# First mixer of a two-block model: logarithms moved behind exponentials, both score maxima taken together, projection jobs spread over other steps, four chunk states made earlier

## What is computed

```python
def gqa_attention(q, k, v):
    ...
    def one_block(qblk):
        s = jnp.einsum('bqkgd,bskd->bkgqs', qblk, k, preferred_element_type=jnp.float32) * scale
        pr = jax.nn.softmax(s, axis=-1)
        return jnp.einsum('bkgqs,bskd->bqkgd', pr.astype(v.dtype), v)
    ...

def gla_chunk_scan(q, k, v, log_f):
    ...
    def step(state, inp):
        qi, ki, vi, gi = inp
        b = jnp.cumsum(gi.astype(jnp.float32), axis=2)
        diff = b[:, :, :, None, :] - b[:, :, None, :, :]
        decay = jnp.exp(jnp.where(lower, diff, -jnp.inf))
        A = jnp.einsum('bhtd,bhsd,bhtsd->bhts', qi.astype(jnp.float32), ki.astype(jnp.float32), decay)
        o_intra = jnp.einsum('bhts,bhse->bhte', A, vi.astype(jnp.float32))
        o_inter = jnp.einsum('bhtd,bhde->bhte', qi.astype(jnp.float32) * jnp.exp(b), state)
        b_last = b[:, :, -1:, :]
        k_dec = ki.astype(jnp.float32) * jnp.exp(b_last - b)
        new_state = state * jnp.exp(b_last[:, :, 0, :])[..., None] + \
            jnp.einsum('bhsd,bhse->bhde', k_dec, vi.astype(jnp.float32))
        return new_state, o_intra + o_inter
    ...

def hgrn2_bidirectional(hq, hf_f, hf_b, hi, hg, lb, out_norm):
    ...
    def gates(fpre, lbd):
        f = lbd + (1.0 - lbd) * jax.nn.sigmoid(fpre.astype(jnp.float32))
        f = f.reshape(B, S, HG_HEADS, HG_DK)
        return 1.0 - f, jnp.log(f)
    ...
```

## Time and profile before

| | us |
|---|---|
| median of 3 runs | 3444.86 |
| the three runs | 3439.9 to 3446.48 |
| the profiled execution, its own time | 3439.18 |
| span of the profiled execution | 3437.3 |
| PE busy | 3080.0 (90%) |
| DVE busy | 2068.4 (60%) |
| ACT busy | 740.9 (22%) |
| POOL busy | 661.1 (19%) |
| the first mixer's attention steps, from the first scores to the last transposes | 157.3 to 310.3 |
| its gated heads, from the first turned keys to the last sum | 345.2 to 506.4 |

### The profile page before, as it was taken

How to read it: one execution, slowest core, us unless ns; L and a number is a source line. 1 busy time by engine, 2 the same in 40 slices (tenths; PEclk the granted TensorE clock), 3 DMA queues, 4 the chain that set the end, 5 groups by cost and what they waited for, 6 DMA issues and landing times. The chain is left out here.

```text
span 3437.3 us, 30881 instructions
## 1 busy us (share of the span) xinstructions
PE 3080.0 (90%) x11312; PEld 1738.6 (51%) x11312; DVE 2068.4 (60%) x4458; ACT 740.9 (22%) x1638; POOL 661.1 (19%) x649
## 2 busy tenths in 40 slices
PE   8999899898888787878777889999999988999998
PEld 3454554433333333333333334536864467878887
DVE  5666731776666777776666318436567777456433
ACT  2134220222222222222222220112111133121000
POOL 0211000344443544444444100000000000000000
PEclk9999899999999999998999999999999999999999
DMA  5765211899999999999999532112235554212222
GB/s 195 250 203 171 74 50 61 329 421 421 421 422 422 417 419 421 413 416 416 418 418 412 222 114 77 49 37 101 86 128 214 209 212 177 78 63 92 91 86 74
DMA packets 118680, 799.23 MB, mean 233 GB/s; under 512 B 13728, under 2 KB 16416, under 8 KB 31872
## 3 DMA queue, kind: packets, MB, share of 16 engines
q0 software_dynamic: 91312, 619.09, 44.7%
q1 hardware_dynamic: 27216, 178.15, 14.5%
HBM read 767.83 MB, written 29.36 MB: 232 GB/s over the span
## 5 line engine op out<-in xcount | busy, mean ns | idle before, releaser
L1312 PE MATMUL po<-pair,diag 128*128 128x512 f32 x2048 | 975.2, 632 | 215.6 <-ACT diag L1395 215.1
L1489 DVE SCALAR_TENSOR_TENSOR pair<-pair,h_tm 128x1024 f32<-128x1024 f32 x512 | 619.2, 1226 | 323.5 <-DMA pair<-in_peer_uv,idx 317.5
L1312 PEld LDWEIGHTS po<-pair,diag 128*128 128x128 f32 x2048 | 404.8, 202 | 758.9 <-issue 473.4
L1205 POOL DMA_INDIRECT pair<-in_peer_uv,idx x512 | 588.7, 1150 | 955.4 <-PE po L1312 661.4
L1388 ACT ACTIVATE ge<-a 128x2 f32<-128x2 f32 (+2 forms) x178 | 36.4, 204 | 930.3 <-DVE pair L1489 930.2
L1911 PE MATMUL acc<-a,ring 128*128 128x512 f32 x512 | 220.9, 592 | 0.0
L1395 ACT ACTIVATE diag<-ident,wt 128x128 f32<-128x128 f32 x512 | 169.1, 392 | 40.9 <-DVE wt L1493 40.9
L1911 PEld LDWEIGHTS acc<-a,ring 128*128 128x128 f32 x512 | 97.3, 190 | 122.0 <-issue 122.0
L1622 PE MATMUL bank<-hT,ring 128*128 128x256 f32 x592 | 139.8, 379 | 0.0
L1622 PE MATMUL bank<-hT,weight_sums 128*128 128x256 f32 x592 | 139.8, 379 | 0.0
L1598 DVE TENSOR_TENSOR weight_sums<-ring 128x512 f32<-128x512 f32 x53 | 36.7, 692 | 168.8 <-DMA ring<-in_w_fc 151.7
(11 more groups left out here) (492 smaller groups left out, 4172.5 us busy)
## 6 DMA issues: line engine op xcount, KB each, us to landing
ring<-in_w_fc SPq DMA_DIRECT2D x62, 1024.0 KB, 4.9
mg<-in_ada_w POOLq DMA_DIRECT2D x96, 512.0 KB, 5.3
tab<-s_tables SPq DMA_DIRECT2D x16, 1664.0 KB, 6.5
ring<-in_w SPq DMA_DIRECT2D x15, 1024.0 KB, 4.9
first<-in_w_first SPq DMA_DIRECT2D x14, 1024.0 KB, 7.7
other<-in_w_first SPq DMA_DIRECT2D x14, 1024.0 KB, 5.0
s_tables<-weight_sums POOLq DMA_DIRECT2D x8, 1664.0 KB, 6.5
s_tables<-table POOLq DMA_DIRECT2D x8, 1664.0 KB, 6.1
```

Of the source, the lines that this page charges most:

```text
L1205: pool.indirect_dma_start(out=pair[:, at, :], out_offset=None, in_=core.dram["peer_uv"][:, :], in_offset=bass.IndirectOffsetOnAxis(ap=idx[ ...
L1312: last = pe.matmul(po[:, t % 2, half * 512:(half + 1) * 512], diag[:, at, :], pair[:, at, D + half * 512:D + (half + 1) * 512], start=firs ...
L1489: dve.scalar_tensor_tensor(row, row, 1.0, h_tm[:, t, :], ALU.mult, ALU.mult, accum_out=a[:, s:s + 1]).then_inc(dotted, 1)
```

## The change

Nothing is added to or taken from the work; only its order changes, in five places.

1. `beside`: the twelve jobs now stand in the steps 0 to 4, 6, 7, 8, 10, 11, 12 and 14; the steps 5, 9 and 13, which have `mix`, and step 15 have none.
2. In the steps with `mix` it stands behind the transposes.
3. ScalarE's two logarithms stand behind the exponentials of units 3 and 5.
4. VectorE takes both maxima of a step first, then one row of `modulate`, both `scale`, and two rows.
5. In the gated heads TensorE makes `key_values(h, 0, 4)` right behind `score(h)`, ahead of the filler job, and VectorE makes `states(h, 0, 4)` right behind `mask(h)`, ahead of the next head's `gates_one`. Two of the four rows of `modulate` ahead of `gates_two(0)` move to heads 0 and 1, one each.

```diff
--- before.py
+++ after.py
@@ -487,7 +487,7 @@
 
         def beside(i):
 
-            return JOB_HV + i - i // 4 - 1 if i % 4 else None
+            return None if i in (5, 9, 13, 15) else JOB_HV + i - sum(i > x for x in (5, 9, 13))
 
         def rows(d, i):
             return (0, GB * (i + 1)) if d == 0 else (GB * i, GC)
@@ -599,11 +599,11 @@
                               start=True, stop=True).then_inc(scored, 1)
                 if beside(i) is not None:
                     job(beside(i))
-                if i >= 5 and i % 4 == 1:
-                    mix(i // 4 - 1)
                 if i:
                     transposes(2 * i - 2)
                     transposes(2 * i - 1)
+                if i >= 5 and i % 4 == 1:
+                    mix(i // 4 - 1)
             transposes(30)
             transposes(31)
             job(JOB_GATE0 + 4)
@@ -685,8 +685,8 @@
                 turn_keys(h)
                 filler(1 if h < 2 else 0)
                 score(h)
+                key_values(h, 0, 4)
                 filler(1)
-                key_values(h, 0, 4)
                 inside(h)
                 filler(1 if h < 2 else 0)
                 key_values(h, 4, NCH - 1)
@@ -742,9 +742,6 @@
                 take(JOB_F + i, kf[:, i // GH, i % GH, :], ACT.Sigmoid).then_inc(taken, 1)
             for h in range(GH):
                 take(JOB_HQ + h, hq[:, h, :], ACT.Silu).then_inc(taken, 1)
-            for d in range(2):
-                act.wait_ge(kept, GH * (d + 1))
-                act.activation(lf[:, d, :, :], lf[:, d, :, :], ACT.Ln).then_inc(logged, 1)
 
             def copy(u):
                 j, a, t = place(u)
@@ -778,6 +775,9 @@
                 act.activation(prob[:, u % 4, :], bank[:, u % 2, :], ACT.Exp, bias=stat[:, 0, u % 8:u % 8 + 1],
                                scale=AD ** -0.5, accum_out=stat[:, 1, u % 8:u % 8 + 1]).then_inc(expd, 1)
                 i = u // 2
+                if u in (3, 5):
+                    act.wait_ge(kept, GH * (u // 2))
+                    act.activation(lf[:, u // 2 - 1, :, :], lf[:, u // 2 - 1, :, :], ACT.Ln).then_inc(logged, 1)
                 if u % 2 and beside(i) is not None:
                     take_later(beside(i))
                 if u % 2 and i:
@@ -939,16 +939,17 @@
                 step(dve.reciprocal(stat[:, 2, u % 8:u % 8 + 1], stat[:, 1, u % 8:u % 8 + 1]))
                 dve.tensor_scalar(prob[:, u % 4, :], prob[:, u % 4, :], stat[:, 2, u % 8:u % 8 + 1], None, ALU.mult).then_inc(scaled, 1)
 
-            for u in range(32):
-                dve.wait_ge(scored, u + 1)
-                if u >= 8:
-                    dve.wait_ge(scaled, u - 7)
-                step(dve.tensor_reduce(stat[:, 0, u % 8:u % 8 + 1], bank[:, u % 2, :], AX.X, ALU.max))
-                dve.tensor_scalar(stat[:, 0, u % 8:u % 8 + 1], stat[:, 0, u % 8:u % 8 + 1], -AD ** -0.5, None, ALU.mult).then_inc(maxed, 1)
-                if u >= 1:
-                    scale(u - 1)
-                modulate(1 + u % 2)
-            scale(31)
+            for i in range(16):
+                for u in (2 * i, 2 * i + 1):
+                    dve.wait_ge(scored, u + 1)
+                    if u >= 8:
+                        dve.wait_ge(scaled, u - 7)
+                    step(dve.tensor_reduce(stat[:, 0, u % 8:u % 8 + 1], bank[:, u % 2, :], AX.X, ALU.max))
+                    dve.tensor_scalar(stat[:, 0, u % 8:u % 8 + 1], stat[:, 0, u % 8:u % 8 + 1], -AD ** -0.5, None, ALU.mult).then_inc(maxed, 1)
+                modulate(1)
+                scale(2 * i)
+                scale(2 * i + 1)
+                modulate(2)
 
             step = Steps(dve, h_step)
 
@@ -1058,19 +1059,18 @@
             dve.memset(kk[:, :, :, :, :], 0.0).then_inc(zeroed, 1)
             dve.wait_ge(zeroed, 2)
             gates_one(0)
-            modulate(4)
+            modulate(2)
             gates_two(0)
             for h in range(GH):
                 mask(h)
+                states(h, 0, 4)
                 if h < 2:
                     up(ups.pop(0))
                 if h + 1 < GH:
                     gates_one(h + 1)
                 if h < 2:
                     up(ups.pop(0))
-                states(h, 0, 4)
-                if h < 2:
-                    modulate(4)
+                    modulate(5)
                     up(ups.pop(0))
                 states(h, 4, NCH - 1)
                 if h + 1 < GH:
```

## The result

The changed kernel takes 3398.7 us (median of 4 runs, 3396.42 to 3403.37) where the kernel before takes 3442.38 beside it: a ratio of 0.9873, 95% interval 0.9861 to 0.9886, so 43.7 us or 1.3% faster. Measured once more with the last experiments, it took 3400.83 against 3441.55, a ratio of 0.9881 (0.9866 to 0.9896), 40.7 us less. The forecast was 3406, 39 us less.

A forecast was written before the change was run, and what follows sets the result against it. TensorE was taken to bound the stage, waits costing idle time and slow-clock matmuls. Attention -21.4 and heads -17.6 make -39.0: from 3439.18 to 3400.2 us, plus 5.7 for the median, 3405.9; range 3395 to 3418.

The forecast's parts named there:

- Attention, -21.4: Attention steps: 152.97 us become 130.1 as TensorE's waits go, less 1.5 for a slow stretch behind step 15; -20.3 to -22.9.
- The way to head 0, -2.3: Ahead of head 0: two fewer VectorE rows cut TensorE's wait for turned keys from 3.49 to 1.2 us.
- Head 0, -1.6: Gated head 0, scores to next scores: 39.4 us become 37.8, with a new wait of 3.1 for late states.
- Head 1, -5.1: Gated head 1: 41.97 us become 36.9, with a 2.6 us wait for `up` and 1.1 of slow job.
- head 2, -7.6: Gated head 2: 40.58 us become 33.0, from a 4.43 us wait and 3.2 of slow clock behind it.
- head 3, -1.0: Gated head 3: its wait of 1.18 us goes, 1.0 us saved.
- A: Gated heads: VectorE takes most of the gain; heads give -8, total -29.4, 3415 us; chance 0.16.
- B: Attention's end and heads: clock stays up, no slow jobs behind waits; total -44 to -46, 3400 us; chance 0.11.
- C: Attention: rows of ada_w arrive late, costing 5 to 7 us; total -33, 3412 us; chance 0.05.
- D: Attention and heads: slower, TensorE stays at 1.2 GHz after a wait; 3452 us if 46 us run slow; chance 0.03.
- E: Whole kernel: nothing changes, because TensorE's idle time comes back in another stage; chance 0.03.

The follow-up runs named there:

- the maxima apart: Changed kernel with VectorE's old order in the attention (maximum, earlier unit's scale, rows of ada_w, unit by unit): 3402.78 us, 0.9893 of the kernel before.
- the jobs as before: Changed kernel with the attention's jobs in their old steps and the mix ahead of the transposes again: 3403.79 us, 0.9887 of the kernel before.
- job 30 in the last step: Changed kernel with job 30 and its ScalarE copy moved ahead of the last two transposes and their copies: 3398.64 us, 0.9867 of the kernel before.
- the attention's edits alone: Kernel before with only the first four of the five edits, gated heads left as they were: 3422.18 us, 0.9952 of the kernel before.

## Why the prediction was right, point by point

- **The place.** It was TensorE's waits ahead of scores and key values, and what was saved on TensorE came out at the end: 39.4 on the touched stretch, 40.7 and 43.7 on medians. The forecast of 3406 lies 7.2 above the 3398.7: 2.5 because the sum took the first median of before (3444.86) as base, where the one beside the changed kernel was 3442.38, 0.4 for the sum itself, and 4.3 outside the touched stretch. That the sum is right to 0.4 is partly luck: the misses below are 2.6 us to the one side and 2.2 to the other.
- **Attention, -21.4.** Measured -21.37. Its parts too: 130.38 for 130.1, step 15's wait 2.49 for 2.7 to 2.8, the mix step 5.66 for 5.62, job 30 slow by 1.2 for 1.5 (with the last transposes, slow as well, 1.8). The argument that a mix step has work enough to cover the chain held. The prediction did not count ScalarE's copies in step 15, the first of which ends some 0.5 us ahead of the scale. The role of the maxima was told incompletely: without them each mix step waits 0.97 for a scale, and step 15 over 2 us more.
- **The way to head 0, -2.3.** Measured -3.87. The wait is 1.20 as forecast; what I had left in the sum was the slow clock behind the old wait of 3.49 (turned keys 1.76 to the next row, now 0.93; job 4.27, now 3.53). Behind a wait of 1.20 the matmuls ran at full speed.
- **Head 0, -1.6.** Measured -0.92, and here the working was off. I had job 37 wait 0.9 for the `up`, behind a slow first job, and then one wait of 3.1 at `across`. With the clock up TensorE was there 2 us earlier, waited 3.22 for the `up`, ran the job slowly (5.27) and then waited 2.09 more for the late states. I had also not seen that five rows in a burst are one more than there are buffers: the fifth waits 0.69 for its transfer (0.53 in head 1), with the `up` and the states behind it. Nor had I the wait of 1.57 ahead of job 39. The new waits of heads 0 and 1 are 8.65 us, for which the prediction's text says 5.0 (its own 0.9, 3.1 and 2.6 make 6.6); the 2 us above that are about what TensorE was earlier.
- **Head 1, -5.1; head 2, -7.6; head 3, -1.0.** Measured -5.34, -7.97 and -1.45. In head 1 the sum is nearer than its parts: the wait was 1.77 for 2.6, with no slow job behind it, where 1.1 was counted, but key values and the first job were 1.6 us slow, which I had not foreseen. Heads 2 and 3 run without idle time, at full clock.
- **Missing.** The output jobs became 1.53 slower: the wait ahead of them is 2.95 in both kernels, and the slow matmuls behind it were 3.1 now and 1.5 before. The sum had no term for it, and the difference is nothing that the change does to these jobs: in the runs with the maxima apart and with the jobs as before, nothing was lost there.
- **Rivals.** A did not come: heads 0 and 1 are bound by VectorE, as it said, but gave 6.3 between them, and head 2 gave all of its gain. (Its own terms give 7.1 for the heads, not 8.) B came for the start of head 0 only. C is seen in the 0.69 and 0.53 of the heads; in the attention rows waited for a transfer once, for 0.20. D: the clock is 1.00 over the attention; denser work brought a higher clock, not a lower one. E: nothing came back but the 1.53 of the output jobs.

By the Trainium skill's rule on transposes (TensorE: Matmul & The Clock Gate, Part 4) the slow job 30 was put down to a stretch of scores, transposes and wait. Transposes and scores alone did not make it slow: the job takes 6.87 with 3 us of scores and transposes and no wait ahead of it (the run with job 30 in the last step), and it is at full speed in the kernel before, behind two groups of transposes and a wait of 0.39. So for such short stretches the wait was needed. Whether the transposes around it lengthen the pause, as the rule would have it, no run here tells.

## What to carry to other kernels

Count, for each step of a software pipeline, the matrix engine's own work against the chain that frees its buffers, and spread the independent jobs so that no step's work is shorter than its chain; a step that has extra work of its own needs no job. Put what another engine waits for ahead of long work that nobody waits for yet (here four states ahead of 10 us of gates), and look at once at what stands behind it, since the next wait was found in the same list. Fill an engine's idle stretches with its background work, in bursts no longer than its buffers.

## What the runs showed of the hardware

The granted clock has a price that differs for one and the same wait. Right behind single waits of 1.56 to 2.06 us matmuls ran at full speed; behind one of 2.20 a job took 8.63 for 6.97. Behind the 2.49 of step 15 the last transposes and job 30 together lost 1.3 to 1.8 us (job 30 took 8.18, 8.15, 7.88, 7.77, 7.69 and 7.48 in six traces, for 6.97). Behind the 3.2 of head 0 the row of four products is 5.25 to 5.40 long in five traces and 6.68 to 6.77 in three, with 3.6 for full speed. Behind the 2.95 ahead of the output jobs 0.1 us was lost in two traces, 1.5 to 1.8 in seven, and 3.0 and 3.1 in the two of the changed kernel:

```profile
477.73 14.00 PE L527 MATMUL acc<-hq,other 128*128 128x512 f32 x32 [2.95 <-DVE hq L1035]
```

That row is of the run with the maxima apart; the changed kernel has 16.99 behind the same 2.95. The longest wait is not the dearest either: scores and job of step 1 lost 2.5 us behind 7.41, 1.7 behind 3.71 and 3.1 behind 2.56. The slow matmuls can also come later: in all seven traces whose head 0 has the waits of 3.2 and 1.57, head 1's key values and first job, behind a job and the short score products, were 1.4 to 3.0 us slow; in the three runs that have only one of the two waits they were not. In the two traces of one and the same kernel, the changed one, every one of these losses repeats to 0.1 us, so it seems to go with where in the program the wait lies rather than with the execution; why it falls out one way or the other, the runs do not show.

The 3.49 ahead of head 0 in the kernel before cost 1.6 us at once and 1.8 more behind the score products; 3.48 in the run with the attention's edits alone cost 1.7 and nothing later.

So a wait of 2.2 to 3.7 us costs 0.1 to 3.4 us on top of itself here, and a sum can have that only as a range. And whether it reaches the end depends on what is next: in head 0, 1.4 us more of slow matmuls in job 37 only shortened the following wait for VectorE.
